# GELUs, gates and V matmuls of two pairs of gathers taken together, one function table for each root, and a new order at both ends

## What is computed

```python
h = h + mixed                       # layer 0: HGRN2 and S5; layer 1: gated DeltaNet
h = h + peer_ffn(rmsnorm(h, ...))   # in both layers

def peer_ffn(xn, w_q, sub_keys, u_tab, v_tab):
    q = (xt @ w_q).reshape(n_tok, 8, 2, 128)
    scores = einsum('thcd,ckd->thck', q, sub_keys)
    top_s, top_i = lax.top_k(scores, 16)
    ...                             # best 16 of the 16 x 16 sums, their experts and softmax gates
    act = gelu(einsum('td,tkd->tk', xb, u_tab[eb]))
    return einsum('tk,tkd->td', gb * act, v_tab[eb])
```

## Time and profile before

| what | value |
|---|---|
| median of 3 runs | 3096.64 us (3095.37 to 3099.3) |
| profiled execution, its own time | 3107.85 us |
| its span, first to last instruction | 3106.1 us |
| mean granted TensorE clock | 0.785 |
| PE busy | 2128.0 us (69%) |
| DVE busy | 2205.4 us (71%) |
| ACT busy | 1466.2 us (47%) |
| POOL busy | 1150.0 us (37%) |
| DMA | 1185.32 MB, mean 382 GB/s |

### The profile page before, as it was taken

The page is one execution under the profiler, slowest core; times in us unless marked ns, Lnnn a source line. Parts: engine busy times, 40 slices in busy tenths (PEclk is TensorE's granted clock), DMA queues, the critical chain, the costliest instruction groups (busy, mean ns, idle before and its releaser), DMA issues.

```text
span 3106.1 us, 39537 instructions
## 1 busy us (share of the span) xinstructions
PE 2128.0 (69%) x13768; PEld 1273.4 (41%) x13768; DVE 2205.4 (71%) x6053; ACT 1466.2 (47%) x3475; POOL 1150.0 (37%) x1041
## 2 busy tenths in 40 slices
PE   7988888674456798877855898987665655453334
PEld 6776454350024575554522566655432411120001
DVE  8646888857777777867576757777866766767763
ACT  3424555433224756785433576778433422242222
POOL 0013334434444434434344333433444443443441
PEclk8889888785568799999877899999876866565555
DMA  5119999999999999989999999999999999999995
GB/s 216 69 57 390 419 419 419 405 378 421 421 420 415 416 392 393 412 318 411 418 420 421 403 362 411 391 412 372 421 420 421 420 421 421 421 421 422 421 421 234
DMA packets 182408, 1185.32 MB, mean 382 GB/s; under 512 B 19648, under 2 KB 25792, under 8 KB 50880
## 3 DMA queue, kind: packets, MB, share of 16 engines
q0 software_dynamic: 147456, 1073.81, 84.0%
q1 hardware_dynamic: 34752, 108.98, 9.1%
HBM read 1180.61 MB, written 2.10 MB: 381 GB/s over the span
## 4 chain that ended last, share of the span: by engine, by line
DMA 41%; PE 29%; ACT 10%; DVE 9%; issue 6%; POOL 4%; another core or an unknown queue 1%; ACTq 0%; SPq 0%; POOLq 0%; DVEq 0%
DMA arena<-uv_tab,cols 40%; PE ps L766 7%; PE xps L694 6%; POOL arena L651 4%; DVE arena L2192 4%; PE ps L694 4%; ACT scr L1433 2%; ACT L1433 2%; PE xps L1126 2%; ACT scr L1437 1%; PE xps L1200 1%; PE xps L1177 1%; PE ps L741 1%; PE xps L1197 1%; DVE arena L2275 1%
## 5 line engine op out<-in xcount | busy, mean ns | idle before, releaser
L651 POOL DMA_INDIRECT arena<-uv_tab,cols x1024 | 1145.9, 1119 | 1900.3 <-PE ps L766 1302.0
L2192 DVE CUSTOM_DVE_ANT_0 arena<-arena 128x1024 f32<-128x1024 f32 x1024 | 1250.6, 1223 | 627.0 <-DMA arena<-uv_tab,cols 598.3
L766 PE MATMUL ps<-arena,scr 128*32 128x512 f32 x4096 | 743.3, 804 | 715.9 <-ACT scr L1437 674.6
L1433 ACT ACTIVATE scr<-sel,cols 128x32 f32<-128x32 f32 x1024 | 273.3, 315 | 1109.6 <-DVE cols L2192 1073.1
L766 PEld LDWEIGHTS ps<-arena,scr 128*32 128x32 f32 x4096 | 93.0, 122 | 1077.0 <-ACT scr L1437 957.3
L694 PE MATMUL xps<-arena,wring 128*128 128x256 f32 x1600 | 394.2, 396 | 14.0 <-ACT arena L1639 5.7
L694 PEld LDWEIGHTS xps<-arena,wring 128*128 128x128 f32 x1600 | 304.8, 198 | 103.8 <-issue 43.7
L694 PE MATMUL ps<-arena,wring 128*128 128x256 f32 x1152 | 288.2, 407 | 4.8 <-DVE arena L1818 4.1
L1437 ACT ACTIVATE scr<-scr,cols 128x32 f32<-128x32 f32 x1024 | 273.0, 313 | 16.6
L694 PEld LDWEIGHTS ps<-arena,wring 128*128 128x128 f32 x1152 | 231.0, 205 | 87.3 <-issue 46.0
L1433 ACT ACT_TABLE_LOAD x158 | 202.7, 1283 | 2.8
(11 more groups left out here) (448 smaller groups left out, 2827.5 us busy)
## 6 DMA issues: line engine op xcount, KB each, us to landing
wring<-wall SPq DMA_DIRECT2D x176, 512.0 KB
arena<-uv_tab,cols POOLq DMA_INDIRECT x1024
arena<-wall SPq DMA_DIRECT2D x16, 512.0 KB, 7.3
h<-xT SPq DMA_DIRECT2D x2, 1024.0 KB, 11.4
arena<-glu_w SPq DMA_DIRECT2D x2, 1024.0 KB, 12.7
out<-arena SPq DMA_DIRECT2D x4, 512.0 KB
arena<-s_b SPq DMA_DIRECT2D x1, 512.0 KB, 8.9
arena<-s_bt SPq DMA_DIRECT2D x1, 512.0 KB, 9.6
```

Source lines behind the costliest of these rows:

```text
L651: pool.indirect_dma_start(out=whole_row(at), out_offset=None, in_=uv_tab, in_offset=bass.IndirectOffsetOnAxis(ap=ids[g % 2][:, k:k + 1], a ...
L766: mm = pe.matmul(ps[4 + half][32 * c:32 * c + 32, :], wdiag[:, b % PAIRS, j, :], pair_row(at + j, 1)[:, T * half:T * half + T], start=(g % ...
L1433: m = act.activation(wdiag[:, b % PAIRS, n % 2, :], place, ACT.Gelu, scale=dots[g % 2][:, n:n + 1])
L2192: dve.tensor_tensor_reduce(u, u, xrep[:, block_of(k), :], 1.0, 0.0, ALU.mult, ALU.add, dots[g % 2][:, k:k + 1]).then_inc(s["dot_done"], 1)
```

## The change

- `gelus` takes four gathers instead of two. It waits for the fourth dot, makes four GELUs, then scales them, and counts `w_ready` after each pair. It stands at k = 4, 8, 12 and, for the last four, at k = 0 of the next round. `values` of both pairs stand together at k = 5, 9, 13 and 1. The gathers' own waits and the ring are as before.
- Every root asks for the table set `natural_log_exp_and_others` ahead of its wait.
- `finish`: the matmuls that bring in `h` are issued before the wait for `y_copied`. In the last tile the second half has a PSUM bank of its own (`ps[0]`), and both residuals come before the wait. The last tile is stored in two halves.
- Front: `soft(0)` stands before `first_query(1)` on ScalarE; `across(0)` stands after two tile rows instead of six; `two_heads` is due at 5.25 (TensorE) and 7.25 (ScalarE) instead of 0.5 and 6, its parts 0.5 steps apart instead of 1.5; the query of round 0 is due one step later.

```diff
+ROOT_SET = "natural_log_exp_and_others"
 def query_at(gi, q):
-    return 16 * r + (8 if r == 0 else 9 if r % 8 == 0 and r > 0 else 2)
+    return 16 * r + (9 if r == 0 else 9 if r % 8 == 0 and r > 0 else 2)
...
 # sync
-            store(2 * TT - 1)
-            sp.wait_ge(s["out_stored"], 16 * TT)
+            for i in range(2):
+                sp.wait_ge(s[("half_normed", "tile_normed")[i]], (1, 2 * TT - 2)[i])
+                sp.dma_start(out[:, 4 * i:4 * i + 4, P * (TT - 1):P * TT],
+                             ysq[:, 4 * i:4 * i + 4, :]).then_inc(s["out_stored"], 16)
+            sp.wait_ge(s["out_stored"], 16 * (TT + 1))
...
 # tensor
             def finish(t, i):
-                side_free(("hy", t, i))
-                if i == 0:
-                    pe.wait_ge(s["y_copied"], t + 1)
+                last = t == 2 * TT - 1
+                def residual(i, o):
+                    for k in range(4 * i, 4 * i + 4):
+                        pe.matmul(o[:, tl(k % 4)], ident[:, :], h[:, k, tl(t % TT)], start=(k % 4 == 0), stop=False,
+                                  skip_group_check=True)
+                o = ps[0] if last and i == 1 else side
+                if not (last and i == 1):
+                    side_free(("hy", t, i))
                 if i < 2:
+                    if not (last and i == 1):
+                        residual(i, o)
+                    if last and i == 0:
+                        residual(1, ps[0])
+                    if i == 0:
+                        pe.wait_ge(s["y_copied"], t + 1)
                     for k in range(4 * i, 4 * i + 4):
-                        pe.matmul(side[:, tl(k % 4)], ycur[:, tl(k)], (ident[:, :], swap)[i], start=(k % 4 == 0), stop=False,
-                                  skip_group_check=True)
-                        mm = pe.matmul(side[:, tl(k % 4)], ident[:, :], h[:, k, tl(t % TT)], start=False,
+                        mm = pe.matmul(o[:, tl(k % 4)], ycur[:, tl(k)], (ident[:, :], swap)[i], start=False,
                                        stop=(k % 4 == 3), skip_group_check=True)
...
             # two_heads
-                            yield 1.5 * (2 * hd + c)
+                            yield 0.5 * (2 * hd + c)
-                yield 6.2
+                yield 3
-            paced += [..., Paced(0.5, two_heads())]
+            paced += [..., Paced(5.25, two_heads())]
...
-            for i in range(6):
+            for i in range(2):
                 first_tile_rows(i)
             across(0)
             first_scores(1)
-            for i in range(6, 8):
+            for i in range(2, 8):
                 first_tile_rows(i)
...
-                    if k == 1 and r:
-                        values(r - 1, 7)
-                    if r < ROUNDS and k > 1 and k % 2 == 1:
-                        values(r, int(k) // 2 - 1)
+                    if k % 4 == 1:
+                        b = int(k) // 2 - 2
+                        for n in (b, b + 1):
+                            if 0 <= PH * r + n < PH * ROUNDS:
+                                values(r + n // PH, n % PH)
...
 # scalar: in norm_root, finish (i == 2), head, first_norm, front, back and out_rows, ahead of the root's wait
+                act.preload_act_table_set(ROOT_SET)
...
             def gelus(g, b):
-                two = range(2 * b, 2 * b + 2)
-                act.wait_ge(s["dot_done"], g * TOPK + 2 * b + 2)
+                four = range(2 * b, 2 * b + 4)
+                act.wait_ge(s["dot_done"], g * TOPK + 2 * b + 4)
                 if 8 * g + b >= PAIRS:
-                    act.wait_ge(s["v_free"], 2 * (8 * g + b - PAIRS) + 2)
+                    act.wait_ge(s["v_free"], 2 * (8 * g + b - PAIRS) + 4)
                 if b == 0:
                     act.wait_ge(s["gate_found"], g + 1)
-                for n in two:
-                    m = act.activation(wdiag[:, b % PAIRS, n % 2, :], place, ACT.Gelu, scale=dots[g % 2][:, n:n + 1])
+                for n in four:
+                    m = act.activation(wdiag[:, n // 2 % PAIRS, n % 2, :], place, ACT.Gelu, scale=dots[g % 2][:, n:n + 1])
                 mark(m)
                 settled()
-                for n in two:
-                    m = act.activation(wdiag[:, b % PAIRS, n % 2, :], wdiag[:, b % PAIRS, n % 2, :], ACT.Copy,
+                for n in four:
+                    m = act.activation(wdiag[:, n // 2 % PAIRS, n % 2, :], wdiag[:, n // 2 % PAIRS, n % 2, :], ACT.Copy,
                                        scale=gate[g % 2][:, n:n + 1])
-                m.then_inc(s["w_ready"], 1)
+                    if n % 2:
+                        m.then_inc(s["w_ready"], 1)
...
+            soft(0)
             first_query(1)
-            for i in range(4):
+            for i in range(2):
                 first_tile_rows(i)
-            soft(0)
             first_scores(1)
-            for i in range(4, 8):
+            for i in range(2, 8):
                 first_tile_rows(i)
...
                     if k == 0 and r:
-                        gelus(r - 1, 7)
-                    if r < ROUNDS and k >= 2 and k % 2 == 0:
-                        gelus(r, int(k) // 2 - 1)
+                        gelus(r - 1, 6)
+                    if r < ROUNDS and k > 0 and k % 4 == 0:
+                        gelus(r, int(k) // 2 - 2)
...
 # vector, tile_done
+                    if t == 2 * TT - 1 and i == 1:
+                        m.then_inc(s["half_normed"], 1)
```

More of the change, by code:

```diff
@@ L534, in trunk @@
             "y_copied", "tile_root",
-            "tile_normed", "small_loaded", "bc_loaded", "glu_loaded", "out_stored",
+            "tile_normed", "half_normed", "small_loaded", "bc_loaded", "glu_loaded", "out_stored",
             "const_pool", "masks_built", "sq_ready", "sum_ready", "root_ready", "hm_ready", "e_mm", "u_ready",
@@ L1284, in _ @@
             paced += [Paced(head_at(g, hd), head(g, hd), g_slot(g)) for g in range(2) for hd in range(HG)]
-            paced += [Paced(-80, first_glu()), Paced(mixed_at(1) + 1, glu(1), g_slot(1)), Paced(0.5, two_heads())]
+            paced += [Paced(-80, first_glu()), Paced(mixed_at(1) + 1, glu(1), g_slot(1)), Paced(5.25, two_heads())]
             paced += [Paced(first_at(m), gates_in(m), spread(m)) for m in range(2)]
@@ L1453, in finish @@
                 if i < 2:
-                    src = side[:, :].rearrange("p (k t) -> p k t", k=4)
+                    src = (ps[0] if t == 2 * TT - 1 and i == 1 else side)[:, :].rearrange("p (k t) -> p k t", k=4)
                     act.activation(h[:, 4 * i:4 * i + 4, tl(t % TT)], src, ACT.Copy)
@@ L1739, in _ @@
             paced += [Paced(head_at(g, hd), head(g, hd), g_slot(g)) for g in range(2) for hd in range(HG)]
-            paced += [Paced(-81.5, first_glu()), Paced(mixed_at(1), glu(1), g_slot(1)), Paced(6, two_heads())]
+            paced += [Paced(-81.5, first_glu()), Paced(mixed_at(1), glu(1), g_slot(1)), Paced(7.25, two_heads())]
             paced += [Paced(first_at(m), gates_in(m), spread(m)) for m in range(2)]
```

## The result

The changed kernel takes 3180.56 us (median of 4 runs, 3171.3 to 3188.56), the one before in the same session 3096.01 (4 runs): a ratio of 1.027 (95% interval 1.024 to 1.0301), 84.5 us slower. I had predicted 3088 and a range of 3045 to 3140. The prediction is wrong in sign and in size, and the rival "the reserve decides" was right in kind but too small.

The account below looks back on a forecast made before the run. The prediction took the kernel as bound by DMA transfers at about 421 GB/s plus DMA idle time. Relief -32, late slots +32, front -3, tail -4.6, other root loads about -1 gave -8.6: from 3096.6 to 3088 us, range 3045 to 3140.

Parts of the forecast that it names:

- the reserve decides: Rival, chance 0.30: in the ring of eight slots 110 busy groups run dry by 0.6 us each; 3130 us (3103 to 3180).
- Slots by fours: Ring of eight: slots returning after each fourth gather cut the reserve from 6.9 to 1.4 us, costing +32 us.
- my upper bound of +86: Ring of eight: the cost in us if every one of the 172 groups ran dry by 0.5 us.
- the two windows that I called calm: 260 to 580 and 660 to 1120 us, at 419 GB/s before the change; late slots costed at nothing in calm stretches.
- The episodes: Starving spells of the DMA: one in each of the first four poor stretches, four from 1840 us; 8 x 4 = +32 us.
- the sign of all this: Windows 260 to 580 and 660 to 1120 us falling from 419 to 400 GB/s or less would show the reserve sized too small.
- Two other signs: Poor stretches: the rate of 291 GB/s at 1340 us should rise above 340, that at 1760 us should fall.
- The relief of ScalarE: Poor stretches: fewer Exp and GELU table loads (73 us together) and ScalarE and TensorE held less often give -32 us.
- The front: Opening: softmax first and two tile rows instead of six bring the first gather forward; -3 us (0 to -6).
- The tail: After the last dot: earlier residuals, no last Exp load and a smaller last store, less the last group's +2.4; -4.6 us.

Follow-up runs that it names:

- experiment 1: Kernel before with only GELUs, gates and value matmuls by fours, all else as before: 3206.15 us, ratio 1.0349.
- six slots: Kernel before, pairs kept, with six slots instead of eight in the ring up to gather 735: 3219.56 us, ratio 1.0392.
- experiment 7: Kernel before with only TensorE's value matmuls by fours, ScalarE keeping its pairs and all its loads: 3171.86 us, ratio 1.0233.
- experiment 6: Changed kernel with pairs up to round 45 and fours only from round 46 on, where the ring has 15 slots: 3074.16 us, ratio 0.9921.
- experiment 3: Kernel before with only the one table set for each root, asked for ahead of the seven waits: 3079.77 us, ratio 0.9942.
- experiment 10: Kernel before with only the order at both ends changed, roots with two tables and pairs kept: 3087.23 us, ratio 0.9968.
- experiment 9: Changed kernel with last table load ahead of its wait, and GELUs, gates and value matmuls gather by gather instead of by fours: 3110.17 us, ratio 1.0038.

## Why the prediction was wrong

**The step that failed** is "Slots by fours": "In a calm stretch 1.4 us are still enough, and I cost it at nothing there", and the +32 that came of it. The same step alone measured +109 (experiment 1), above even my upper bound of +86. The path from the fourth dot to the issue (5.2 sized, 5.1 seen) and the cover (9.95) were right. Wrong was the point at which the reserve ends. I put it at zero, with 3.3 us from an issue to its first data taken from the opening (5.8 us from issue to dot), where the DMA was empty; in the stream the same way took 8.0 us in the group shown, and it varies. The reissued gather came 0.66 us late with 1.4 us in hand, so the point lies near 2 us; six slots, with 1.9, stand right at it (0.8 us lost in 32 pairs). By the prediction's own formula, t(1 - g/421), the two windows that I called calm have lost 43 us instead of 4: 39 us where I had nothing. Only a part of that is calm in the strict sense. Over gathers 192 to 256 the dots fall back by 0.43 us for each group in experiment 1, and by 0.28 in the changed kernel itself. Spread over all 180 groups that would be 50 to 77 us. It is an estimate and an extrapolation from one stretch.

**The episodes**, eight of 4 us each, were too few as well. Six slots lose 0.8 us in gathers 192 to 256 and 122 us in all (4 of them at the change of the ring), so a reserve that is 5 us smaller costs over 100 us where the engines are late; TensorE's order alone costs 73 there. I had taken the windows under 400 GB/s as the places where the full reserve ran out, and counted only those; most busy places used part of it and showed 415 to 420. I had named the sign of all this: 260 to 580 and 660 to 1120 at 400 or less. They came out at 395 and 400. Six slots brought the same windows to 396 and 403, so the sign tells that the reserve was too small, and not whether it failed in calm or in busy places. Two other signs failed: the stretch at 1340 came to 324, not above 340, and that at 1760, which should have fallen, rose from 351 to 385 (with other work in it by then).

**The relief of ScalarE** came as far as the loads go; what the GELUs' part of it is worth in time was not shown. The Exp loads are gone, the GELU loads from 260 to 2160 us are 94 (100 predicted):

```profile
L1451 ACT ACT_TABLE_LOAD x94 | 120.6, 1283 | 1.7
...
L1659 ACT ACT_TABLE_LOAD x14 | 18.0, 1283 | 0.3
...
L1742 ACT ACT_TABLE_LOAD x6 | 7.7, 1283 | 0.1
```

L1659 and L1742 are the loads ahead of the Ln; the Exps' lines have none. The slower kernel has fewer gathers in that stretch, so a part of the 94 is no saving: experiment 7, in which ScalarE's program is as before, has 121 there. Over the whole kernel the loads ahead of the GELUs fall from 158 to 126. ScalarE's busy time is 168 us less. Of the -32, the roots bring -17 by themselves, a third of it in the opening, where I had counted 1 us for all loads outside the stretch. The GELUs' half brought nothing that its own delay didn't take back: with slots to spare the grouping changes nothing (experiment 6), without them ScalarE's half is a net +34 (1 less 7). VectorE's wait for the root fell from 55.6 us to 34 with the roots alone (experiment 3) and to 6.3 with both. The first step, with the gathers on time, is relief. The second need not be: six slots alone, with all loads in place, bring it to 9.9.

**The front** (-3 sized) measured -6.4 on the first dot (experiment 10), with the tile rows not slowed; my 0 to -6 was too timid on `soft(0)`: TensorE reached `across(0)` at 212.2 with the ends alone and at 210.4 in the changed kernel, not 215. **The tail** (-4.6 sized) measured -4.1, with the last load exposed; with it hidden, and in pairs, it is -6.9. Both steps held.

**The rivals.** "The reserve decides" (chance 0.30) had the mechanism, but priced 110 busy groups at 0.6 us and calm ones at nothing, 3130 with an upper end of 3180; the measured 3180.56 lies just above it.

## What to carry to other kernels

Where a ring of buffers feeds a saturated DMA, the reserve (cover of what is in flight less the time from landing to new data) has no safe small value: against 6.9 us here, 4.4 cost 1% and 1.9 cost 4%. A kernel that seems calm at 419 GB/s may be using most of it. Price any edit that holds buffers longer by every group that passes through the ring, calm ones first, take the delay of a reissue from the middle of the stream and not from its start, and scale the price by a run with one buffer less, which needs one line. Batching to save an engine's overhead is worth having only where that engine, and not the return of buffers, ends the wait; don't read a smaller wait in a slower kernel as relief before a run without the relief has been looked at; and a root's load is best asked for ahead of every wait, the last one too.

## What the runs showed of the hardware

The value matmuls of a pair run beside each other. Eight records of them (two gathers) take 1.94 us; the four records of one gather issued alone take 1.92 us, in the timeline of experiment 9:

```profile
758.90 1.92 PE L769 MATMUL ps<-arena,scr 128*32 128x512 f32 x4 [0.58 <-ACT scr L1450]
```
